# Experts with three sets of raw weights, a ring of five pieces and one block a turn; q and k normed after the rotation; small loads moved

## The reference

```python
qf = rmsnorm(q.reshape(B, S, H, 2, dh), q_g)        # dh = 64, k likewise
qf = apply_rope(qf, cos, sin) * (dh ** -0.5)
...
# top group, then the top 2 of its 8 experts; 32 experts, 2048 x 2 rows
padded = (counts + MOE_BLOCK - 1) // MOE_BLOCK * MOE_BLOCK      # MOE_BLOCK = 128
...
def run_block(args):                                 # xblk: 128 rows of one expert
    xblk, e = args
    return (jax.nn.silu(xblk @ w1[e]) * (xblk @ w3[e])) @ w2[e]
```

## Time and profile before

| | before |
|---|---|
| median of 3 runs | 3572.6 us |
| the profiled execution, its own time | 3581.5 us |
| its span | 3579.6 us |
| PE busy | 2910.6 us (81%) |
| DVE busy | 2178.4 us (61%) |
| ACT busy | 1561.0 us (44%) |
| POOL busy | 864.5 us (24%) |

### The profile page before, as it was taken

The page is one execution under the profiler, slowest core; times in us unless marked ns, Lnnn a source line. Parts: engine busy times, 40 slices in busy tenths (PEclk is TensorE's granted clock), DMA queues, the critical chain, the costliest instruction groups (busy, mean ns, idle before and its releaser), DMA issues. The chain is left out here.

```text
span 3579.6 us, 42731 instructions
## 1 busy us (share of the span) xinstructions
PE 2910.6 (81%) x13766; PEld 2292.2 (64%) x13766; DVE 2178.4 (61%) x2930; ACT 1561.0 (44%) x2415; POOL 864.5 (24%) x438
## 2 busy tenths in 40 slices
PE   2699897899999978889958889806898899999850
PEld 2566665676767666777747768705776677777740
DVE  5556675454544555433636542236798799999866
ACT  4212221454545543222333321205676677887751
POOL 3000000000000001110100011134665667676652
PEclk8899998999999998888989999957999999999985
DMA  5263314333333344111169955207867866756628
GB/s 196 92 223 140 99 59 128 112 98 109 103 104 106 92 153 160 48 38 44 54 228 288 295 191 212 95 4 258 297 244 277 306 233 247 263 207 223 243 98 318
DMA packets 338556, 598.28 MB, mean 167 GB/s; under 512 B 36057, under 2 KB 138713, under 8 KB 334466
## 3 DMA queue, kind: packets, MB, share of 16 engines
q1 hardware_dynamic: 310386, 527.23, 42.9%
q0 software_dynamic: 13040, 43.61, 3.4%
q10 hardware_dynamic: 15008, 25.85, 1.9%
HBM read 434.56 MB, written 162.07 MB: 167 GB/s over the span
## 5 line engine op out<-in xcount | busy, mean ns | idle before, releaser
L2568 DVE TENSOR_TENSOR moe_w_lo<-moe_W,moe_w_hi 128x1024 fp32r<-128x1024 f32 x300 | 537.9, 1831 | 144.0 <-ACT moe_w_hi L2495 143.9
L2495 ACT CAST moe_w_hi<-moe_W 128x1024 fp32r x400 | 409.5, 1050 | 262.0 <-SPq L2415 89.9
L2640 POOL TENSOR_TENSOR moe_w_lo<-moe_W,moe_w_hi 128x1024 fp32r<-128x1024 f32 x100 | 262.4, 2624 | 279.5 <-ACT moe_w_hi L2495 279.5
L2646 POOL TENSOR_TENSOR moe_w_lo<-moe_W,moe_w_hi 128x1024 fp32r<-128x1024 f32 x98 | 288.9, 2961 | 61.8 <-ACT moe_w_hi L2502 54.9
L951 POOL MEMSET pooling_pw<- 128x256 f32 x1 | 0.3, 313 | 1201.6 <-POOLq L138 1201.6
L2574 DVE TENSOR_TENSOR moe_w_lo<-moe_W,moe_w_hi 128x1024 fp32r<-128x1024 f32 x98 | 252.8, 2595 | 19.6 <-ACT moe_w_hi L2502 17.2
L2444 PE MATMUL moe_h1b<-moe_w_hi,moe_xT_hi 128*128 128x512 f32 x392 | 171.0, 436 | 89.8 <-DVE moe_xT_lo L2580 89.8
L2502 ACT CAST moe_w_hi<-moe_W 128x1024 fp32r x192 | 194.7, 1049 | 69.0 <-PE moe_h1b L2446 56.8
L1675 PE MATMUL project_bank<-h_lo,w_hi 128*128 128x512 f32 x512 | 205.1, 401 | 0.0
L702 DVE TENSOR_SCALAR_CACHE_REDUCE att_S<-att_bank 128x512 f32<-128x512 f32 x192 | 125.0, 689 | 125.8 <-PE att_bank L485 125.8
L518 PE MATMUL att_bank<-h_hi,w_hi 128*128 128x512 f32 x384 | 173.3, 451 | 9.9 <-PEq L138 6.6
(11 more groups left out here) (452 smaller groups left out, 7388.5 us busy)
## 6 DMA issues: line engine op xcount, KB each, us to landing
moe_W<-in_moe_w SPq DMA_DIRECT2D x96, 2048.0 KB, 10.4
ybuf<-moe_y ACTq DMA_DIRECT2D x49, 512.0 KB
w_raw<-in_gate_w SPq DMA_DIRECT2D x48, 512.0 KB, 3.8
out_sg<-gateT SPq DMA_DIRECT2D x32, 768.0 KB, 8.2
ybuf<-att_zero SPq DMA_DIRECT2D x36, 512.0 KB, 6.6
gateT<-att_gates SPq DMA_DIRECT2D x48, 256.0 KB, 2.4
gateT<-gate_out SPq DMA_DIRECT2D x48, 256.0 KB, 2.3
front_w<-in_ada_w SPq DMA_DIRECT2D x8, 1024.0 KB, 7.6
```

What stands on the lines that cost most here:

```text
L2495: nc.scalar.copy(w_hi[:, at, :], raw(e, p)).then_inc(q["w13_high"], 1)
L2568: nc.vector.tensor_tensor(w_lo[:, at, :], raw(e, p), w_hi[:, at, :].bitcast(F32), ALU.subtract).then_inc(q["w13_low_dve"], 1)
L2640: nc.gpsimd.tensor_tensor(w_lo[:, at, :], raw(e, p), w_hi[:, at, :].bitcast(F32), ALU.subtract).then_inc(q["w13_low_pool"], 1)
L2646: nc.gpsimd.tensor_tensor(w_lo[:, at, :], raw(e, p), w_hi[:, at, :].bitcast(F32), ALU.subtract).then_inc(q["w2_low_pool"], 1)
```

## The change

It has four parts.

**Small loads.** The six loads of attention (gain, four lambda vectors, gate bias) are issued on ACT's queue at the start of project, and pooling takes the same gate bias tile. In pooling the late halves are issued first, ua after them.

```diff
-                act.dma_start(gcol[:, 0:1], g["subln_g"].rearrange("a n -> n a"), allow_slow_non_contiguous=True).then_inc(q["small"], 16)
-                for j, n in enumerate(("lambda_q1", "lambda_k1", "lambda_q2", "lambda_k2")):
-                    act.dma_start(lq[:, j], g[n].broadcast_to([P, DH])).then_inc(q["small"], 16)
-                act.dma_start(gb[:], g["gate_b"].rearrange("a (k p) -> p (a k)", p=P),
-                               allow_slow_non_contiguous=True).then_inc(q["small"], 16)
...
-                sp.dma_start(ua[:, 0, :], g["zT"][0]).then_inc(u_ready[0], 16)
-                sp.dma_start(tiles["gb"][:], g["gate_b"].rearrange("a (k p) -> p (a k)", p=P),
-                             allow_slow_non_contiguous=True).then_inc(small, 16)
-                sp.dma_start(ua[:, 1, :], g["zT"][1]).then_inc(u_ready[1], 16)
                 sp.dma_start(h_hi[1][:].bitcast(F32), g["late_hi"][:, :, 512:1024]).then_inc(h_ready, 16)
                 sp.dma_start(h_lo[1][:].bitcast(F32), g["late_lo"][:, :, 512:1024]).then_inc(h_ready, 16)
+                for c in range(2):
+                    sp.dma_start(ua[:, c, :], g["zT"][c]).then_inc(u_ready[c], 16)
```

```diff
+                def swap(n):
+
+                    m = order[n]
+                    if m >= 2:
+                        act.wait_ge(q["roped"], m - 1)
+                    for to in range(0, P, 32):
+                        nc.scalar.copy(other2[to:to + 32, m % 2, :], bank[n % 4][to ^ 32:(to ^ 32) + 32, :]).then_inc(q["swapped"], 1)
...
+                    if n >= 2 and not is_z[n - 2]:
+                        high(n - 2)
...
+                        dve.wait_ge(q["q_split"], m - 1)
+                    nc.vector.tensor_tensor(o[:, m % 2, :], qn2[:, m % 2, :], rs2[:, m % 2, :], ALU.mult).then_inc(q["normed"], 1)
...
+                    dve.wait_ge(q["swapped"], 4 * m + 4)
+                    nc.vector.scalar_tensor_tensor(own, bank[n % 4][:], gcol[:, j:j + 1], cos[:, at], ALU.mult, ALU.mult).then_inc(q["turned"], 1)
+                    link(nc.vector.scalar_tensor_tensor(other, other, gcol[:, 2 + j:3 + j], sin[:, at], ALU.mult, ALU.mult))
+                    dve.wait_ge(q["turned"], m + 1)
+                    nc.vector.tensor_tensor(own, own, other, ALU.add).then_inc(q["roped"], 1)
```

```diff
+                def turn_over(e, u, before, before_times):
+
+                    end = sp.value_load(r["blk"][0:1, bass.ds(e + (96 - SLOTS), 1)], min_val=1, max_val=64)
+                    sp.wait_ge(q["w1_low"], end * 4)
+                    sp.sem_inc(q["go"], 1)
+                    load("w1", e, u)
+                    arrived("w1", before, before_times)
+                    sp.wait_ge(q["w3_low"], end * 4)
+                    sp.sem_inc(q["go"], 1)
+                    load("w3", e, u)
+                    arrived("w3", before, before_times)
+                    sp.wait_ge(q["block_done"], end)
+                    sp.sem_inc(q["go"], 1)
+                    load("w2", e, u)
+                    arrived("w2", before, before_times)
+                sp.dma_start(ident[:], g["const_pack"][:, CONSTS["ident"][0]:CONSTS["ident"][1]]).then_inc(q["ident_ready"], 16)
+                for u in range(SLOTS):
+                    for n in parts:
+                        load(n, u, u)
+                for n in parts:
+                    arrived(n, 0, 1)
+                full = NE // SLOTS
+                with sp.Fori(1, full) as i:
...
+                            if k < KS:
+                                pe.matmul(yb[nh][:], hT_hi[:, k, :], w_hi[:, at, part], start=k == 0, stop=False)
+                                pe.matmul(yb[nh][:], hT_hi[:, k, :], w_lo[:, at, part], start=False, stop=False)
+                                mm = pe.matmul(yb[nh][:], hT_lo[:, k, :], w_hi[:, at, part], start=False, stop=False)
+                            else:
+                                mm = pe.matmul(yb[nh][:], hT[:, k - KS, :], W[:, bass.ds(at_raw + (2 * W13 + k * D + nh * 512), 512)],
+                                               start=False, stop=k == KF - 1)
+                        if k < KS:
+                            mm.then_inc(q["used"], 1)
+                    mm.then_inc(q["block_done"], 1)
...
+                    b = i + 1
+                    at, e = place(act, b - 1), expert(act, b - 1)
+                    high_2(b - 1, at, e, 0)
+                    gate(b)
+                    high_2(b - 1, at, e, 1)
+                    at, e = place(act, b + 1), expert(act, b + 1)
+                    high_13(b + 1, at, e, range(0, 3))
+                    place_x(b + 1)
+                    high_13(b + 1, at, e, range(3, R))
+                    place_y(b - 1)
+                    place_h(b)
+                    high_13(b + 1, at, e, range(R, P13))
...
+                    b = i + 1
+                    at = place(dve, b - 1)
+                    low_2(b - 1, at, 0)
+                    silu(b)
+                    low_2(b - 1, at, 1)
+                    at = place(dve, b + 1)
+                    low_13(b + 1, at, range(0, 2))
+                    hidden(b)
+                    low_13(b + 1, at, range(2, 3))
+                    split_x(b + 1)
+                    low_13(b + 1, at, range(3, R))
+                    split_h(b)
+                    low_13(b + 1, at, range(R, P13))
```

More of the change, by code:

```diff
@@ L1679, in _ @@
                         mean(n - 1)
-                    if n >= 2 and not is_z[n - 2]:
-                        rotate(n - 2)
             @block.scalar
@@ L1732, in _ @@
                         root(n - 1)
-                    if n >= 2 and not is_z[n - 2]:
-                        high(n - 2)
+                    if n < NU and not is_z[n]:
+                        swap(n)
             @block.vector
@@ L1811, in _ @@
                         sum_ada(m)
+                    if 1 <= n <= NU and not is_z[n - 1]:
+                        norm(n - 1)
                     if n < NU and not is_z[n]:
-                        norm(n)
-                    if n >= 2 and not is_z[n - 2]:
-                        low(n - 2)
-                    if 1 <= n <= NU and not is_z[n - 1]:
-                        rope(n - 1)
+                        rope(n)
         s.end()
@@ L2529, in _ @@
+                count = blocks_left(act)
                 act.sem_inc(q["y_placed"], 2)
[L2530 to L2536 removed]
+                act.sem_inc(q["stored"], 16)
+                high_13(0, 0, 0, range(R), first=True)
@@ L2559, in _ @@
+                at, e = place(act, count), expert(act, count)
+                for k in range(P2):
+                    high_2(count, at, e, k)
+                place_y(count)
+                act.wait_ge(q["stored"], count * 16 + 32)
                 act.sem_inc(q["finished"], 1)
@@ L2607, in _ @@
+                count = blocks_left(dve)
+                low_13(0, 0, range(R), first=True)
+                split_x(0)
+                low_13(0, 0, range(R, P13), first=True)
+                at = place(dve, 1)
+                low_13(1, at, range(0, 1))
+                silu(0)
+                low_13(1, at, range(1, 2))
                 hidden(0, True)
-                low_13(1, 1, e, range(7, 8))
-                split_x(1, 1)
+                low_13(1, at, range(2, 3))
+                split_x(1)
@@ L2625, in _, with gather @@
+                    low_13(b + 1, at, range(3, R))
+                    split_h(b)
+                    low_13(b + 1, at, range(R, P13))
+                at = place(dve, count)
+                for k in range(P2):
+                    low_2(count, at, k)
             @block.gpsimd
             def _(pool):
-                def gather(b, n, par):
-                    pool.wait_ge(q["x_turned"], b + 1)
-                    nc.gpsimd.tensor_copy(idx[par][:], r["slot_tok"][:, bass.ds(b, 1)]).then_inc(q["idx_copied"], 1)
+                def gather(b, first=False):
+                    if not first:
+                        pool.wait_ge(q["x_turned"], b)
+                    nc.gpsimd.tensor_copy(idx[:], r["slot_tok"][:, bass.ds(b, 1)]).then_inc(q["idx_copied"], 1)
```

443 lines of the change are left out of this document (183 added, 260 removed).

## The result

| | median | runs |
|---|---|---|
| before | 3574.6 us | 6 |
| after | 3591.3 us | 6 |

The ratio is 1.0047 with a 95% interval of 1.0034 to 1.0060. The kernel is slower, by 17 us where 33 were forecast: 3591.3 us for 3606, inside the range of 3550 to 3650. The profiled execution of after took 3593.5 us with a span of 3591.8.

The account below looks back on a forecast made before the run. TensorE, busy 81% of the span, was taken as held up by waits in projection, attention, pooling and experts. Terms 88 - 14 - 6 - 35 = 33 us on a median of 3572.6 gave 3606 us, range 3550 to 3650.

Parts of the forecast that it names:

- step 5: Experts: the weight signal stands behind the wait for block_done, so 16 single-block turns take 29.2 us each, others 19.2.
- step 6: Experts' start: nine loads issued before the first signal put the first cast at 2454 for 2430.86, first product 2463 for 2439.
- step 4: Experts: a block without other waits takes 19.2 us by PE's work, against 19.16 before.
- step 3: Projection, q and k: the late norm cuts a unit from 8.79 to 7.7 us, despite GpSimd delaying DVE; gain 35 us.
- the circle: Projection, q and k, before: DVE's add, ACT's high part, square and root, then DVE again; 8.79 us a unit.
- step 1: Attention's start: bias, lambda and gain loads moved to the projection's start gain 14 us (5 to 18).
- step 2: Pooling's start: late halves issued ahead of ua take 6 us (0 to 9) off a 13.50 us wait.
- rival B: Experts: the signal doesn't gate, a single-block turn costs 19.2 us and the time is 3446 us; chance 0.10.
- Rival A: Projection: GpSimd and DVE don't collide, 38 us less, 3568 us; chance 0.14.
- C: Experts: a late gathered x or late casts cost 1 us in each of 47 turns, 3653 us; chance 0.06.
- D: Attention and pooling: the moved loads gain nothing since another load holds both, 20 us more, 3626 us; chance 0.10.

## Why the prediction was right, point by point

**The signal (step 5).** The mechanism was read from the order of SP's program, and one run shows it by itself: its 172 us go when only the signals move. The parts of a turn, forecast and in the turn from 2480.70: SP from the last w2 product to the cast 2.2 and 2.85 us; cast to the next first product 6.6 and 6.62; together with PE's own work and its clock 29.2 and 30.6. Over the 16 turns the mean is 28.8 us; the first of a row is 27.3 to 28.0, since PE enters it with its clock up (1.00 granted from 2657.1 to 2680.9, in the first of the row of seven), the later ones 28.5 to 30.6. The turn behind a row is 20.1 to 21.5 us for the same reason. The 16 turns took 460 us where 467 stood. The other 30 behind the first took 577 us, 19.2 each as forecast; this was luck, two errors that cancel, since an ordinary turn is 18.7 us and the long ones behind a stall make up for it. From the first product to the last store it was 1091 us for 1090.

**The start (step 6).** The first product came 22 us later relative to the stage than before (2387.06 and, 74.3 us earlier for the stages ahead, 2439.03), 24 were forecast. That SP's queue takes only so much and then holds SP itself was read from one row, 6.30 us in the earlier trace rows. The nine issues bear it out: the first two took 0.4 and 0.6 us, the other seven 2.6 to 9.5 us each, and all nine 40.4 us.

**PE's work of a turn (step 4).** 18.7 us against 19.2. The four float32 products take 3.59 us with their tail, as worked out. What was overpriced is the value read on PE's queue: I took 0.35 us for it, and the turns are 18.73 us, 0.1 less than the sum without it (18.83).

**The late norm (step 3): right in kind, too small.** 51 us in the stage for 35. POOL meets one operation of DVE as forecast, but takes 0.96 us from it instead of 1.2: 7.13 + 1.15/4 = 7.42 us for 7.7. That alone would give (8.79 - 7.42) x 32 = 44 us, and from the first to the last reciprocal it is 44 us less (293 before, 249 after), but not by this sum. Before, some units next to a break were shorter than 8.79, and the 29 usual distances (without the one in the middle of the stage and the one behind the burst of stores) were 8.59 us on average, after 7.40: 35 us. Another 8.6 us lie in the distance in the middle, 29.42 us before and 20.83 after, and 7.8 behind the last reciprocal, 19.7 and 11.9. So the units gave what was forecast, and the circle also stood at two places that the sum had no term for.

**Attention (step 1): 24 us for 14.** At the start the gain is 15 us for the 14 forecast (from the first product to the one after v is turned over, 31.3 before and 16.1 after). Nine more us lie further on. 2.7 us come right behind the start, where before's clock, at its lower level since the wait, comes up only at 643.8. The rest comes in four steps of about 1.5 us, without a wait that is longer in before than in after. At the first of these steps the rows show a granted clock of 0.94 before and 1.00 after:

```profile
874.00:902.30 28.30, 24.47 (x154) 17.94 (x152) 15.44 (x44) 15.07 (x30) 0.00 (x0) 0.94 0.03 10
...
805.60:832.30 26.70, 22.87 (x153) 16.89 (x152) 15.44 (x44) 15.04 (x30) 0.00 (x0) 1.00 0.03 11
...
879.40:882.60 3.20, 3.20 (x11) 2.38 (x13) 1.31 (x4) 1.82 (x4) 0.00 (x0) 0.50 0.00 0
...
730.00:1243.00 513.00, 479.19 (x2911) 365.71 (x2909) 256.79 (x705) 268.90 (x539) 0.00 (x0) 1.00 0.34 109
```

The first row is of before, the second of after, for the same 150 or so matmuls: 28.3 and 26.7 us. The third is of before: inside that stretch the clock is at its lower level, with PE busy all the time. It falls like this five times in before's attention behind the start (at 794, 879, 968, 1053 and 1142) and once in after's (at 725); the fourth row has after's clock up from there to the stage's end. The run with only the late norm has the clock of after here, one fall (at 740), and is 8 us shorter than before in this stage, though its attention is that of before. So the falls don't belong to the loads; they may belong to when the stage begins. Why the clock falls in one case and not in the other isn't settled; no run here was made for it.

**Pooling (step 2).** 3 us for 6. The wait for the late half is shorter by 6.5 us, as thought, but ua is late in its place, 2.95 us.

**The sum.** -71 for the three parts in one run, -55 forecast; +85 for the experts, +88 forecast. So the net figure was missed by gains ahead of the experts that the sum priced too low: the two places in the projection and the clock in attention. The forecast's one large doubt was whether anything covers SP's wait; rival B held that something might, and nothing does. Rival A (no collision) fell by the add of 1.66 us, C by turns of 18.7, D by PE's rows at both starts.

## What to carry to other kernels

Where one engine both waits for a buffer to come free and passes on that other buffers are full, write down for each signal which wait stands ahead of it: loading three experts ahead gained nothing while the signal of weights that had landed 48 us before stood after a wait for the newest work, and moving the signals ahead of that wait was worth 172 us. Issue a first batch of loads so that the first signal isn't behind the last load: nine issues held SP 40 us here. And when a faster stage doesn't get faster in time, look at the longest distance in it and not the usual one: here one burst of stores took back half of what the unit had won.

## What was not expected of the hardware

- The DMA engines moved 343 GB/s over 131 us while TensorE worked all the time, and 398 GB/s over 73 us where the loads bound the turns. The 334 GB/s on which I had based an expectation was what a stretch asked for, not what is there.
- A GpSimd subtraction of 512 columns took 1.30 us (at 411.80 in after) while DVE stood idle and 1.74 us when it began inside DVE's scaled product, and DVE's add behind it became 0.96 us longer. The scaled product kept its 0.74 us. The two operations nearly went one behind the other: from the product's end at 404.12 to the add's at 405.81 are 1.69 us, for 1.30 and 0.69 alone. So an operation of 1.3 us cost 0.44 us on one engine and 0.96 on the other.
- Attention became 8 us shorter, its granted clock 0.98 for 0.97, when only the stage before it had been changed. The clock fell five times there in the kernel before, with PE busy, and once in this run.
